# Delta rule: in-place selection instead of mask additions, and another placing of its small steps among the weight products

## The chip, the cores and the metric

The kernel runs on one core of one Trainium2 chip. The metric is the device time of one execution in microseconds. The kernel before takes 3056.31 us (median of three runs, 3056.17 to 3056.36).

## The reference, cut to what matters

Two layers of a hybrid encoder trunk over 256 frames of width 2048, all in float32. Layer 0 mixes forgetting attention and a convolution module, layer 1 is a gated delta rule; each is followed by a SwiGLU feed-forward part. The change touches layer 1 alone. There, for 16 query/key heads and 32 value heads of width 128:

```
q = l2_normalize(q) * HEAD_DIM ** -0.5        # x * rsqrt(sum(x * x) + 1e-6)
k = l2_normalize(k)
decay = exp(where(tril, gcum[:, None] - gcum[None, :], -inf))
lower = where(strict, (k * beta) @ k.T * decay, 0)
a_mat = lower + eye(CHUNK)                    # unit lower triangular
sol   = triangular_solve(a_mat, rhs)
intra = (q @ k.T) * decay
```

## The kernel before, in words

**The weight stream.** Nearly all of the time goes into products with weights from HBM (some 490 MB). They are walked in groups of 512 output columns, each group in four chunks of 1 MB. For each chunk SyncE loads `raw` (L402), ScalarE rounds it in two halves to the short float `w_hi` (L556), VectorE subtracts to get the rest `w_lo` (L902), and TensorE does 16 wide products of `w_hi` with both parts of the activations (L1664) and 16 narrow ones of `w_lo` (L1657). `w_hi` and `w_lo` have two buffers, so the `w_hi` of chunk c + 2 waits until TensorE is through with chunk c. After a group ScalarE copies the second half of each of four accumulators to `tmp` (L563) and VectorE adds the first half (L908); TensorE waits for these sums before it overwrites the accumulators in the next group. For the groups that carry queries, keys and values of the delta rule VectorE then scales by the norm (L967) and does the short convolution in eight portions of two operations (L992, L994), and ScalarE takes the SiLU (L721).

**The delta rule beside it.** The heads are taken in four sets (0 to 3) of four query/key heads and eight value heads. While set j is computed, the stream works through six groups, the gate `z` of set j and the projections of set j + 1 (for set 3 the output projection). Each engine has a generator for the delta rule (`gdn_act`, `gdn_dve`, `gdn_pool`, `gdn_pe`) that is resumed six times in each chunk, so 24 times a group and 144 times a set, at fixed places in the engine's own program; `yield from upto(clock, n)` lets what follows run at the resumption after n. These numbers are called steps below. On TensorE four of the six lie after the 4th, 8th, 12th and 16th wide product, two after the 8th and 16th narrow one (in the last chunk of a group the order is halved: wide, narrow, wide, narrow of eight each). ScalarE and VectorE have their first two steps around the second half of the next chunk's `w_hi` and `w_lo`, the others after it, in the last chunk among the sums. No engine reorders anything: a step that waits holds up everything behind it on its engine.

**What a set does**, with the steps before the change. ScalarE squares queries and keys (L824). TensorE sums the squares over the partitions by products with ones into four PSUM tiles (L1768, steps 4 and 5). ScalarE, in one piece at step 5, takes four logarithms (L830) and one exponential of the whole tile (L834), which makes the reciprocal roots; both need their table loaded. VectorE multiplies queries (step 12), then keys (13) by them (L1321). GpSimd has meanwhile fetched the gate rows, broadcast over the partitions, into `L` and `I` (two DMAs, L1507, 1.5 MB each, after the outputs of the set before were saved), cleared `XT` (L1509), and adds masks of large numbers to two thirds of either (L1512, L1514: four operations of 128x1024). ScalarE takes exponentials of `L` (steps 16 to 23; L841, L842) and `I` (from 24; L851). TensorE makes the products of keys with keys (from step 17; L1776, L1777) and keys with queries (L1860, L1861), VectorE multiplies them into `L` (from 19; L1329, L1331) and `I` (from 28; L1341). GpSimd clears `Xb` and `XTb` (L1517, L1518), moves the diagonal 32x32 blocks of `L` through DRAM to a layout with one block per partition (L1528, L1532), and VectorE inverts them there (`invert`, steps 38 to 62): small operations up to blocks of 16 (L1419 to L1465), then eight large ones of 128x1024 (L1474, L1478, L1483, L1487), one in each step, and a copy (L1492). GpSimd takes the inverses back through DRAM (L1537, L1544, from step 60), VectorE transposes them (L1360, steps 84 to 87), and TensorE works the blocks up to 64 and 128 and finishes the set (from L1805, step 88). VectorE's last product writes the outputs into `zs` (L1398, steps 131 to 134); GpSimd saves them (L1549). For set 3 the saved outputs of the other sets come back as input of the output projection (`og_upper` L586 on ScalarE, `og_lower` L975 on VectorE).

## Time and profile before

| | |
|---|---|
| median of three runs | 3056.31 us (3056.17 to 3056.36) |
| the profiled execution | 3057.1 us, of which its span is 3055.4 us |
| mean granted clock of TensorE | 0.955 |
| TensorE (products) busy | 2817 us, 92% of the span |
| VectorE busy | 1952 us, 64% |
| ScalarE busy | 1402 us, 46% |
| GpSimd busy | 642 us, 21% |
| read from HBM | 491.6 MB, 164 GB/s over the span |

Times in the trace are microseconds from the start of the span. PE is TensorE, PEld its weight loads, DVE VectorE, ACT ScalarE, POOL GpSimd. A row of the timeline merges equal neighbours: start, time from the first's start to the last's end, engine, line, operation, `out<-in`, shapes, count, and in square brackets the idle time before it and what ended it. `x16` is sixteen instructions. PEclk is the granted clock as a share of full speed: 1.00 is 2.4 GHz, 0.50 is 1.2 GHz. The delta rule's four sets run from about 1372 to 2189 us.

### The profile page before, as it was taken

To read this page: it belongs to the slowest core of one execution; us is meant where nothing else is said; L and a number is where in the kernel's file an instruction comes from. 1 tells how busy PE (TensorE), PEld (TensorE's weight loads), DVE (VectorE), ACT (ScalarE), POOL (GpSimd) and SP (SyncE) were. 2 spreads that over 40 slices of the span, in tenths; PEclk is the share of its full clock that TensorE was granted. 3 is DMA by queue.
4 is the path that set the end of the run, shared out by engine and by line. 5 is a ranking of instruction groups with operands and counts; after the bars stand their busy time and mean duration, and the time that the engine had idled before them with its cause. 6 is when DMAs were issued, how large, how long until landed. Compare 5 with 4: busy or idle time off the path is not lost. (4 is left out here: it accounts for less than half of the span.)

```text
span 3055.4 us, 43790 instructions
## 1 busy us (share of the span) xinstructions
PE 2817.2 (92%) x15973; PEld 2463.7 (81%) x15973; DVE 1951.9 (64%) x2454; ACT 1402.3 (46%) x2142; POOL 642.0 (21%) x549
## 2 busy tenths in 40 slices
PE   6966889999999999999888988979899999999997
PEld 5855668888888888877777877968788888888886
DVE  4599647555555555687767668677476555555555
ACT  3555434444444444456355453463444444444443
POOL 4054014011111112411021020031142101210214
PEclk8988879999999999999999999999999999999998
DMA  5533225555555555554444345354455555555553
GB/s 170 165 110 110 97 69 182 191 192 191 181 193 192 185 188 180 172 193 136 131 165 151 119 174 157 120 194 149 139 188 185 187 192 188 186 191 193 181 177 110
DMA packets 246088, 502.26 MB, mean 164 GB/s; under 512 B 10919, under 2 KB 11528, under 8 KB 244392
## 3 DMA queue, kind: packets, MB, share of 16 engines
q1 hardware_dynamic: 237232, 473.99, 47.7%
q0 software_dynamic: 5888, 25.79, 2.4%
q8 instruction: 97, 1.59, 0.2%
q10 hardware_dynamic: 2808, 0.38, 0.1%
q14 instruction: 63, 0.52, 0.0%
HBM read 491.64 MB, written 8.49 MB: 164 GB/s over the span
## 5 line engine op out<-in xcount | busy, mean ns | idle before, releaser
L902 DVE TENSOR_TENSOR w_lo<-raw,w_hi 128x1024 fp32r<-128x1024 f32 (+1 forms) x912 | 1165.9, 1312 | 770.8 <-ACT w_hi L556 770.1
L1664 PE MATMUL acc<-xs,w_hi 128*128 128x512 f32 x5248 | 1333.4, 402 | 59.8 <-ACT w_hi L556 24.3
L556 ACT ACTIVATE w_hi<-raw 128x1024 fp32r<-128x1024 f32 (+1 forms) x912 | 905.4, 1036 | 1011.1 <-PE acc L1657 1002.7
L1664 PEld LDWEIGHTS acc<-xs,w_hi 128*128 128x128 f32 x5248 | 979.1, 194 | 253.2 <-issue 43.4
L1657 PE MATMUL acc<-xs,w_lo 128*128 128x256 f32 x5248 | 719.4, 288 | 63.9 <-DVE w_lo L902 63.9
L1657 PEld LDWEIGHTS acc<-xs,w_lo 128*128 128x128 f32 x5248 | 692.6, 194 | 99.6 <-DVE w_lo L902 70.0
L1664 PE MATMUL acc<-hs,w_hi 128*128 128x512 f32 x1920 | 468.8, 393 | 15.4 <-issue 11.4
L1664 PEld LDWEIGHTS acc<-hs,w_hi 128*128 128x128 f32 x1920 | 352.2, 189 | 83.2 <-issue 13.0
L563 ACT ACTIVATE tmp<-acc 128x256 f32<-128x256 f32 x456 | 172.4, 382 | 338.4 <-PE acc L1657 285.6
L1657 PEld LDWEIGHTS acc<-hs,w_lo 128*128 128x128 f32 x1920 | 251.4, 191 | 12.5
L1657 PE MATMUL acc<-hs,w_lo 128*128 128x256 f32 x1920 | 255.3, 283 | 0.0
L485 POOL TENSOR_TENSOR ut<-gt,ut 128x1024 f32<-128x1024 f32 x22 | 52.9, 2406 | 837.8 <-DVE ut L967 837.8
L908 DVE TENSOR_TENSOR ut<-acc,tmp 128x256 f32<-128x256 f32 x336 | 135.3, 421 | 142.0 <-ACT tmp L563 138.1
L463 POOL TENSOR_TENSOR xT<-xT,ut 128x256 f32 (+1 forms) x140 | 104.1, 766 | 493.9 <-DVE ut L908 493.8
L1219 DVE SCALAR_TENSOR_TENSOR conv<-u_pad,conv_w,conv 128x256 f32<-128x256 f32 x120 | 100.3, 900 | 0.0
L994 DVE SCALAR_TENSOR_TENSOR gt<-ut,short_w,gt 128x255 f32<-128x255 f32 (+2 forms) x192 | 96.9, 563 | 0.2
L1255 POOL TENSOR_TENSOR conv<-conv,prod 128x1024 f32<-128x1024 f32 x30 | 80.2, 2674 | 62.6 <-ACT prod L1244 56.1
L474 POOL TENSOR_TENSOR sq_acc<-sq_acc,sq_one 128x256 f32<-128x256 f32 x60 | 68.8, 1147 | 4.7
L493 POOL TENSOR_TENSOR hs<-ut,hs 128x1024 f32 (+1 forms) x22 | 68.2, 3102 | 5.4 <-POOL hs L490 5.4
L1549 POOL DMA_DIRECT2D og_save<-zs x4 | 3.7, 913 | 295.4 <-DVE zs L1398 295.4
L472 POOL TENSOR_TENSOR sq_one<-xT 128x256 f32 (+1 forms) x60 | 63.6, 1061 | 7.6 <-POOL sq_acc L474 4.1
L908 DVE TENSOR_TENSOR gt<-acc,tmp 128x256 f32<-128x256 f32 x96 | 38.4, 421 | 34.5 <-ACT tmp L563 33.2
(290 smaller groups left out, 1650.4 us busy)
## 6 DMA issues: line engine op xcount, KB each, us to landing
raw<-in_w_in SPq DMA_DIRECT2D x136, 1024.0 KB, 5.2
raw<-in_w_gate SPq DMA_DIRECT2D x88, 1024.0 KB, 5.2
raw<-in_w_up SPq DMA_DIRECT2D x88, 1024.0 KB, 5.2
raw<-in_w_down SPq DMA_DIRECT2D x64, 1024.0 KB, 5.1
raw<-in_w_out SPq DMA_DIRECT2D x48, 1024.0 KB, 5.2
raw<-in_w_down SPq DMA_DIRECT2D x32, 768.0 KB, 4.5
L<-g_rows POOLq DMA_DIRECT2D x4, 1536.0 KB, 7.9
I<-g_rows POOLq DMA_DIRECT2D x4, 1536.0 KB, 11.6
```

The source lines that it names most:

```text
L463: nc.gpsimd.tensor_tensor(row, row, ut[:, m], ALU.add).then_inc(resid_added, 1)
L474: nc.gpsimd.tensor_tensor(sq_acc[:], sq_acc[:], sq_one[:], ALU.add).then_inc(sq_added, 1)
L493: nc.gpsimd.tensor_tensor(hb[:, bass.ds(4 * i, 4), 1, :], ut[:], hi.bitcast(F32), ALU.subtract).then_inc(h_ready, 1)
L556: nc.scalar.activation(w_hi[:, c % 2, k], raw[:, c, k], ACT.Copy).then_inc(hi_ready, 1)
L563: nc.scalar.activation(tmp[:, m % 2], acc[:, m, T:2 * T], ACT.Copy).then_inc(tmp_ready, 1)
L902: nc.vector.tensor_tensor(w_lo[:, c % 2, k], raw[:, c, k], w_hi[:, c % 2, k].bitcast(F32), ALU.subtract).then_inc(lo_ready, 1)
L908: nc.vector.tensor_tensor(dst, acc[:, m, 0:T], tmp[:, m % 2], ALU.add).then_inc(acc_free, 1)
L994: last = nc.vector.scalar_tensor_tensor(gt[:, m, s:T], ut[:, m, 0:T - s], w, gt[:, m, s:T], ALU.mult, ALU.add)
L1219: return eng.scalar_tensor_tensor(conv[:, ct], u_pad[:, ct, k:k + T], w, conv[:, ct], ALU.mult, ALU.add)
L1255: nc.gpsimd.tensor_tensor(conv[:, CONV_DVE:], conv[:, CONV_DVE:], prod[:, k % 2], ALU.add)\
L1657: last = mm(acc[:, m, T:2 * T], w_lo[:, c % 2, k, cols], r[:, kk, 0], start=False, stop=end, skip_group_check=True)
L1664: mm(acc[:, m, :], w_hi[:, c % 2, k, cols], r[:, kk], start=kk == 0, stop=end, skip_group_check=True)
```

## The change

Four things change in the delta rule; all data and results stay where they were.

1. GpSimd selects in place instead of adding masks: `affine_select` over eight heads at a time keeps the triangle and fills the rest with the large number. One operation replaces one addition, four in a set. The constant `mask_up` goes, with its memset and its select at the start.
2. On ScalarE the four logarithms have a step each (8 to 11), and the exponential is split into keys (step 13) and queries (step 14). VectorE multiplies keys at step 15 and queries at step 16, each behind its own half. TensorE's first products of keys are at step 18 instead of 17.
3. In the inverse each of the eight large operations has two steps; the inverse has 33 steps instead of 25 and starts at step 40 instead of 38.
4. What follows is placed two steps later on all engines (the exponentials of `L` and the products into `L` one step). Two places keep their steps: GpSimd's way back through DRAM (60) and VectorE's transposes (84).

The diff, without the hunks that only add 2 to the number in `upto(clock, ...)`:

```
-        mask_up = sb("mask_up", [P, P])
...
-            link(pool.memset(mask_up[:], 0.0))
-            select(mask_up[:], [[1, P]], 0, -1, fill=NEG)
...
             nc.scalar.activation(qk_sq[:], qk_in[:], ACT.Square).then_inc(l2_act, 1)
-            yield from upto(clock, 5)
-
-            act.wait_ge(l2_pe, j + 1)
             for n in range(4):
+                yield from upto(clock, 8 + n)
+                act.wait_ge(l2_pe, j + 1)
                 q = n < 2
                 nc.scalar.activation(qk_sq[:, n // 2, 2 * (n % 2):2 * (n % 2) + 2, :].rearrange("p a t -> p (a t)"),
                                      aux[n][:], ACT.Ln, bias=eps[:, 1:2] if q else eps[:, 0:1],
                                      scale=float(P) if q else 1.0).then_inc(l2_act, 1)
-            act.wait_ge(l2_act, 6 * j + 5)
-            nc.scalar.activation(qk_sq[:], qk_sq[:], ACT.Exp, scale=-0.5).then_inc(l2_act, 1)
+            for n, h in enumerate((1, 0)):
+                yield from upto(clock, 13 + n)
+                act.wait_ge(l2_act, 7 * j + 5)
+                nc.scalar.activation(qk_sq[:, h], qk_sq[:, h], ACT.Exp, scale=-0.5).then_inc(l2_act, 1)
 
             for h in range(SV):
-                yield from upto(clock, 16 + h)
+                yield from upto(clock, 17 + h)
...
         def gdn_dve(dve, j):
...
-            for h in range(2):
-                yield from upto(clock, 12 + h)
-                dve.wait_ge(l2_act, 6 * j + 6)
+            for n, h in enumerate((1, 0)):
+                yield from upto(clock, 15 + n)
+                dve.wait_ge(l2_act, 7 * j + 6 + n)
                 nc.vector.tensor_tensor(qk_in[:, h], qk_in[:, h], qk_sq[:, h], ALU.mult).then_inc(l2_dve, 1)
             for a in range(SQ):
-                yield from upto(clock, 19 + 2 * a)
+                yield from upto(clock, 20 + 2 * a)
...
-            yield from upto(clock, 38)
+            yield from upto(clock, 40)
             for n in range(N_TICKS):
                 next(inverse)
-                if 46 <= clock[0] < 50:
-                    a = clock[0] - 46
+                if 48 <= clock[0] < 52:
+                    a = clock[0] - 48
...
                 link(nc.vector.tensor_tensor(pr, ath[:, 4 * n:4 * n + 4].unsqueeze(2).to_broadcast([P, 4, 16, 16]),
                                              square(Lb, 16, 0, 16).unsqueeze(1).to_broadcast([P, 4, 16, 16]), ALU.mult))
                 yield
+                yield
                 ready()
                 link(nc.vector.tensor_reduce(pt[:, 4 * n:4 * n + 4], pr, AX.X, ALU.add))
+                yield
                 yield
...
             pool.wait_ge(rows_in, 32 * j + 32)
-            for n in (0, 2):
-                nc.gpsimd.tensor_tensor(L[:, :, n], L[:, :, n], over_heads(mask_fox[:]), ALU.subtract).then_inc(gd_pool, 1)
-            for n, mask in ((0, mask_up), (2, mask_up)):
-                nc.gpsimd.tensor_tensor(I[:, :, n], I[:, :, n], over_heads(mask[:]), ALU.add).then_inc(gd_pool, 1)
+            apart(pool)
+            for t, fill, sign in ((L, -NEG, 1), (I, NEG, -1)):
+                for n in (0, 2):
+                    pool.affine_select(out=t[:, :, n], in_=t[:, :, n], compare_op=ALU.is_ge, fill=fill, base=0,
+                                       pattern=[[0, SV], [-sign, P]], channel_multiplier=sign).then_inc(gd_pool, 1)
...
         def gdn_pe(pe, mm, tr, j):
...
             for a in range(SQ):
-                yield from upto(clock, 17 + 2 * a)
+                yield from upto(clock, 18 + 2 * a)
                 pe.wait_ge(l2_dve, 2 * j + 2)
...
             for a in range(2, SQ):
-                yield from upto(clock, 21 + 2 * a)
+                yield from upto(clock, 22 + 2 * a)
                 scores(pe, mm, j, a)
...
-N_CONST = 11
+N_CONST = 9
...
-N_TICKS = 7 + 1 + 3 + 3 + 1 + 1 + 8 + 1
+N_TICKS = 7 + 1 + 3 + 3 + 1 + 1 + 16 + 1
```

The second pair of large operations (L1483, L1487) gets its two further `yield` in the same way.

## Rows read from the trace of the kernel before

**Rows 1.** The page, second part: granted clock of TensorE in 40 slices of 76 us.

```profile
PEclk8988879999999999999999999999999999999998
```

**Rows 2.** Four sets: length; PE, PEld, DVE, ACT, POOL busy; clock, DMA share, GB/s.

```profile
1371.87:1568.68 196.81, 181.55 (x1074) 158.89 (x1073) 143.14 (x239) 100.87 (x187) 14.64 (x22) 0.96 0.43 136
1568.68:1778.96 210.28, 183.56 (x1075) 159.76 (x1073) 154.71 (x244) 101.59 (x188) 28.41 (x29) 0.94 0.46 151
1778.96:1984.90 205.94, 186.21 (x1072) 162.26 (x1073) 145.61 (x237) 100.58 (x185) 27.98 (x29) 0.93 0.45 146
1984.90:2188.90 204.00, 180.10 (x1074) 156.98 (x1072) 138.79 (x196) 100.99 (x187) 40.63 (x43) 0.95 0.50 166
```

**Rows 3.** Timeline of TensorE in set 0, from the inverse to the first use of it.

```profile
1438.93 2.12 PE L1664 MATMUL acc<-xs,w_hi 128*128 128x512 f32 x8 [1.56 <-DVE ut L908]
...
1463.79 2.08 PE L1657 MATMUL acc<-xs,w_lo 128*128 128x256 f32 x8 [4.02 <-DVE w_lo L902]
...
1475.42 3.82 PE L1664 MATMUL acc<-xs,w_hi 128*128 128x512 f32 x16
...
1488.43 1.33 PE L1805 MATMUL aux<-XT,L 128*128 128x64 f32 x8 [2.68 <-DVE X L1360]
```

**Rows 4.** TensorE's waits, 1360 to 2206 us: total, times, longest.

```profile
PE acc L1657 <- DVE w_lo L902: 25.4, 9, 5.5
PE aux L1776 <- DVE qk_in L1321: 23.8, 4, 10.7
PE acc L1664 <- issue: 17.5, 2, 11.4
PE aux L1805 <- DVE X L1360: 9.4, 4, 2.7
PE acc L1664 <- ACT w_hi L556: 8.2, 4, 2.1
PE acc L1664 <- DVE ut L908: 8.1, 6, 2.3
PE aux L1860 <- DVE L L1331: 3.3, 4, 2.1
```

**Rows 5.** Timeline of GpSimd, masks of set 1 and a clearing.

```profile
1585.86 5.88 POOL L1512 TENSOR_TENSOR L<-L,mask_fox 128x1024 f32<-128x1024 f32 x2 [10.09 <-DMA I<-g_rows]
1591.70 5.01 POOL L1514 TENSOR_TENSOR I<-I,mask_up 128x1024 f32<-128x1024 f32 x2
1602.52 0.95 POOL L1517 MEMSET Xb<- 128x1024 f32 x1 [5.81 <-DVE qk_in L1321]
```

**Rows 6.** Timeline of VectorE, the same place in set 0 (first two) and set 1.

```profile
1387.70 2.36 DVE L902 TENSOR_TENSOR w_lo<-raw,w_hi 128x1024 fp32r<-128x1024 f32 x2 [7.97 <-ACT w_hi L556]
1389.98 3.24 DVE L994 SCALAR_TENSOR_TENSOR gt<-ut,short_w,gt 128x255 f32<-128x255 f32 x8
...
1584.90 4.57 DVE L902 TENSOR_TENSOR w_lo<-raw,w_hi 128x1024 fp32r<-128x1024 f32 x2 [7.05 <-ACT w_hi L556]
1589.40 9.56 DVE L994 SCALAR_TENSOR_TENSOR gt<-ut,short_w,gt 128x255 f32<-128x255 f32 x8
```

**Rows 7.** GpSimd's selects at the start (L422): count, ns, start.

```profile
L422 POOL TENSOR_SCALAR_AFFINE_SELECT mask_up<-mask_up x1: 292/292/292, 3.8 to 3.8; 128x128 f32<-128x128 f32 x1
```

**Rows 8.** Groups of GpSimd by shape: count, busy us, mean ns, idle before.

```profile
L490 POOL CAST hs<-ut 128x1024 f32 x16 | 27.5, 1720 | 4.2 <-POOL ut L485 4.2
```

**Rows 9.** Timeline of VectorE beside such a CAST (568.65 to 570.36).

```profile
567.69 3.74 DVE L902 TENSOR_TENSOR w_lo<-raw,w_hi 128x1024 fp32r<-128x1024 f32 x2 [1.79 <-ACT w_hi L556]
```

**Rows 10.** Timeline of ScalarE in set 1, the exponential.

```profile
1580.72 1.28 ACT L834 ACT_TABLE_LOAD   x1
1582.02 1.91 ACT L834 ACTIVATE qk_sq<-qk_sq 128x2048 f32<-128x2048 f32 x1
```

**Rows 11.** Timeline of VectorE in set 0, last copy of the inverse.

```profile
1463.65 0.45 DVE L1492 COPY XTb<-rms 64x128 f32<-64x128 f32 x2
```

**Rows 12.** Transfers of the inverse back to `XT` (L1544).

```profile
DMA to landing us min/median/max: 2.5/3.3/5.9
```

More of the change, by code:

```diff
@@ L845, in gdn_act @@
             for h in range(SV):
-                yield from upto(clock, 24 + (3 * h) // 2)
+                yield from upto(clock, 26 + (3 * h) // 2)
                 if h == 0:
@@ L871, in gdn_act @@
             for a in range(SQ):
-                yield from upto(clock, 120 + a)
+                yield from upto(clock, 122 + a)
                 act.wait_ge(gd_pe[a], NP * j + P_O)
@@ L877, in gdn_act @@
                 last.then_inc(gd_act[a], 1)
-            yield from upto(clock, 125)
+            yield from upto(clock, 127)
             all_heads(act, gd_act, NA * (j + 1))
@@ L1362, in gdn_dve @@
             for a in range(SQ):
-                yield from upto(clock, 94 + a)
+                yield from upto(clock, 96 + a)
                 dve.wait_ge(gd_pe[a], NP * j + P_Z5)
@@ L1381, in gdn_dve @@
             for a in range(SQ):
-                yield from upto(clock, 112 + a)
+                yield from upto(clock, 114 + a)
                 dve.wait_ge(gd_pe[a], NP * j + P_P)
@@ L1387, in gdn_dve @@
             for a in range(SQ):
-                yield from upto(clock, 127 + a)
+                yield from upto(clock, 129 + a)
                 dve.wait_ge(gd_pe[a], NP * j + P_O)
@@ L1765, in gdn_pe @@
             yield from upto(clock, 4)
[L1766 removed]
+            pe.wait_ge(l2_act, 7 * j + 1)
             for n in range(4):
@@ L1789, in gdn_pe @@
             for a in range(SQ):
-                yield from upto(clock, 44 + a)
+                yield from upto(clock, 46 + a)
                 pe.wait_ge(gd_act[a], NA * j + A_LT)
@@ L1797, in gdn_pe @@
             for a in range(SQ):
-                yield from upto(clock, 88 + a)
+                yield from upto(clock, 90 + a)
                 pe.wait_ge(inv_dve, N_INV * j + N_INV)
@@ L1807, in gdn_pe @@
             for a in range(SQ):
-                yield from upto(clock, 92 + a)
+                yield from upto(clock, 94 + a)
                 pe.wait_ge(gd_act[a], NA * j + A_Y5)
@@ L1811, in gdn_pe @@
             for a in range(SQ):
-                yield from upto(clock, 98 + a)
+                yield from upto(clock, 100 + a)
                 pe.wait_ge(gd_dve[a], ND * j + D_X5)
@@ L1819, in gdn_pe @@
             for a in range(SQ):
-                yield from upto(clock, 102 + a)
+                yield from upto(clock, 104 + a)
                 pe.wait_ge(gd_act[a], NA * j + A_Y6)
@@ L1823, in gdn_pe @@
             for a in range(SQ):
-                yield from upto(clock, 106 + a)
+                yield from upto(clock, 108 + a)
                 pe.wait_ge(gd_dve[a], ND * j + D_X6)
```

29 lines of the change are left out of this document (14 added, 15 removed).

## The prediction

> **What bounds the kernel now.** I read the page first: TensorE's granted clock is below full in the first quarter and then, after a steady stretch, through the middle of the span [rows 1], where the delta rule runs. I then cut the stretch of the delta rule, four sets of heads, into windows: each takes 197 to 210 us, and the clock averages 0.93 to 0.96 in them [rows 2]. A set is 24 chunks of weights, and a chunk alone takes TensorE 5.6 us (16 wide products take 3.82 us [rows 3], 16 narrow ones 1.9 us more, less overlap), so some 134 us of each set are weights, the rest is the delta rule's own products and waiting. The seven longest lines of TensorE's waits over this stretch [rows 4] hold 96 us, among them 23.8 us before L1776 (the first product after normalisation), 25.4 us for `w_lo` from VectorE, 8.2 us for `w_hi` from ScalarE, 9.4 us before L1805, 17.5 us of "issue". What the lower clock costs: one minus the clock times the busy time of each set [rows 2] is 7.3 + 11.0 + 13.0 + 9.0 = 40 us, so each us of waiting brings with it 40/96 = 0.4 us of slow matmuls. I use that as a factor. Memory is no bound (DMA share 0.43 to 0.50 [rows 2]).
>
> Two causes stand behind the waits. One is GpSimd: while its four mask additions run (1585.86 to 1596.7 in set 1 [rows 5]), VectorE's second `w_lo` and its short convolution stretch: 9.56 us for eight operations that take 3.24 us in set 0, 4.57 us for two `w_lo` that take 2.36 us there [rows 6]. That is 8.5 us, and in front of L1776 TensorE sat 10.7 us in that set [rows 4]. The other is VectorE itself: in the inverse it is packed without a gap, and the time from 1438.93 to 1463.79 is VectorE's own work, with TensorE waiting 4.02 us at its end [rows 3].
>
> **The change, part by part.**
>
> *Start.* Two constants fewer on GpSimd (a memset and a select of 0.29 us [rows 7], under 0.7 us with their gaps) in GpSimd's first 4.4 us, while the constants' DMAs keep TensorE waiting for longer: nothing, and if that cover were gone, 0.7 us.
>
> *Masks.* Four TENSOR_TENSOR of 128x1024, some 2.7 us each [rows 5], become four selects of one input. The trace has selects of 128x128 only, 0.29 us [rows 7]; a one-input CAST of 128x1024 takes 1.72 us [rows 8]. Bounds for one select: below, the memset's 0.95 us [rows 5]; above, eight times 0.29 = 2.3 us, near a mask addition's shortest. I take the CAST, same size and one input. The trace shows that a CAST holds up VectorE as an addition does (the pair of `w_lo` at 567.69, beside an addition's last 0.7 us and a CAST, takes 3.74 us [rows 9] instead of 2.36), while `w_lo` beside the memset of 1602.52 kept its 1.2 us. The Trainium skill's page "SBUF — State Buffer", section "Who interferes with whom", says the same in a rule that speaks against this change: a VectorE instruction with two SBUF inputs contends with any GpSimd instruction that reads SBUF, and the lock is held for the whole instruction; by it a select still blocks, only for less time. The Trainium skill's "GPSIMD Engine Reference", section "Engine selection", has one-input operations run at roughly line rate, by which a select would take an estimated 1 us instead of 1.7 and the kernel's time would come out near that of the first rival below.
> In set 0 the masks run during the last group before the stretch, and cost TensorE a wait for `w_lo` of 4.7 us (one of the nine in the first line of [rows 4]). With 4 x 1.7 us instead of some 11, VectorE ends its convolution some 2.5 us sooner: gain 2.5 us.
>
> *Logarithms, exponentials, normalisation.* Today all four logarithms and the exponential stand in one block after chunk 0, ahead of the `w_hi` of chunk 2: TensorE waits 2.1 us four times (8.2 us [rows 4]). With logarithms in steps 8 to 11, both halves of that `w_hi` are out first: this wait goes. What is late next: the new chain through chunk 2 begins when TensorE ends chunk 1 and frees the buffer: `w_hi` 1.05, table load 1.28, exponential of the keys 1.0 (half of 1.91 [rows 10] and a fixed part), `w_hi` 1.05, `w_lo` 1.2, two taps 0.8 [rows 6], product of the keys 1.21, two taps 0.8, product of the queries 1.21: 9.6 us. TensorE is at its new step (18) after 5.57 + 1.0 = 6.6 us. So a wait of 3.0 us is left before L1776 even with GpSimd silent; nothing gets faster there, since the products moved three steps later on VectorE and the user only one on TensorE. Queued behind the wait are the weights of chunk 3; behind ScalarE's new waits stand only later `w_hi` with room to spare. Splitting the exponential adds 0.2 us of ScalarE, hidden.
> In sets 1 to 3 the selects begin 14 to 17 us after the set's start, as the masks do now (the row DMAs gate them), and this chain runs 15 to 25 us after it. So they no longer meet a convolution with slack, but the chain itself. Two of four falling on it add 3.4 us (from 0 to 4 x 1.72 possible). New waits: 3.0 + 3 x 6.4 = 22.2 us against 8.2 + 23.8 + 3.3 (L1860, which starts one step later with its operands no later) = 35.3 us [rows 4]: gain 13.1 us.
> Clock on these 15.6 us of waits: 0.4 x 15.6 = 6.3 us.
>
> *Inverse.* The eight large operations (1.22 us each) get two steps each, the whole starts two steps later, the last copy ten steps later. The work is the same and VectorE sets the pace, so little vanishes: stepping through chunks, steps 49 to 72 hold 31 us of VectorE for 22 us of TensorE. Today TensorE reaches the second chunk of the next group (1475.42) 40.2 us after it entered the stretch (1435.2, which is 1438.93 less the wait and eight products before it [rows 3]); placed by the new steps I get waits of 1.2, 1.9, 1.2, 0.6 and 1.9 us and 35.7 us, 4.5 us better, because VectorE no longer idles behind its own late `w_lo` and the small operations start the sums earlier. But the inverse itself ends at 33 us instead of 28.9 (1463.65 and 0.45 [rows 11]): **4 us later**. From there the blocks go through DRAM; GpSimd's waits and issues take 9 us of that, the last landing 3.3 us (up to 5.9) more [rows 12], some 13 us together. VectorE then stands at its step 84 waiting 1.6 to 3.4 us, with `w_lo` of the next chunk queued behind, and L1805 starts at 51.7 to 53.5 us, two steps (1.9 us) further on in the work than today's 53.2 (1488.43 [rows 3]): a net 1.6 to 3.4 us. I take 2.5 us for sets 0 to 2, clock included. In set 3 the two loads of stored heads stand between (6.0 us of the "issue" line of [rows 4] at the first): gain at the first of them, loss at the second, 0 in all.
>
> *Everything after moves by two steps*, on all engines alike. That is free until the end of a set: the last product with `zs` gates the save of the heads, GpSimd's. In sets 1 to 3 the row DMAs and selects start some 1.5 us later (counted above), and after set 3 the chain of save, load, ScalarE and VectorE that ends TensorE's longest "issue" wait, 11.4 us [rows 4], starts and ends about 1 us later: loss 1 us.
>
> **Sum.** 2.5 + 13.1 + 6.3 + 3 x 2.5 - 1 = 28.4 us. The profiled execution took 3057.1 us (span 3055.4), which gives 3028.7 us; the median of the runs stands 0.8 us below it: **3028 us**, 0.9% faster. A measurement of this kernel can tell about 0.2%, 6 us, from no change.
>
> **Rivals.**
> *The lock costs nothing* (20%): selects as short as the memset's 0.95 us [rows 5], mostly between VectorE's operations. Waits 4 x 3.0 = 12 us, gain 23.3; nearly all of the 4.7 us before set 0, 4.3; clock 0.4 x 27.6 = 11; inverse 3 x 4.5 if the blocks land early; less 1: 51 us, 3005 us. For: GpSimd's memsets disturb no one. Against: the CAST does.
> *Selects scale with their columns* (18%): 8 x 0.29 = 2.3 us each, that is 0.6 us more for up to four blocked operations in four places, with the clock 1.4 x 16 x 0.6 = 13 us: 3042 us.
> *The blocks' way through DRAM becomes the bound* (13%): landings of 5.9 us, waits of 5.5 us at L1805 with slow matmuls behind: the 7.5 us are gone and 3 more: 3039 us. GpSimd's code being fetched anew before the first select of a set would land near 3045 us. The start of the trace speaks against that: its selects follow their memsets within 0.3 us.
> *Slower* (7%): a select over eight heads in a strided tile takes a slow path and holds the lock all through. Each us above 1.7 costs 1.4 x 16 = 22 us; from 3.0 us a select the gain is gone, at 3.5 us the kernel takes 3067 us. Against: 0.29 us for 128 columns.
> *It does nothing* (4%): a packed VectorE merely passes its lateness on to another line: 3056 us.
> The forecast's own case has 38%. Range for eight in ten: 3005 to 3048 us, which leaves out the fast half of the first rival and the last two. Faster by over 0.2%: 0.88; within: 0.05; slower: 0.07.
>
> **What would show it.** GpSimd's selects near 1.7 us; no 2.06 us waits for `w_hi`; waits before L1776 of about 3 us in set 0 and 5 to 7 us in sets 1 to 3, with taps or the product at 2 us instead of 0.4 and 1.2; the last copy of the inverse 4 us later against the group's start, and VectorE waiting for a DMA before L1360; set lengths falling by about 7 us on average, set 1 most. The forecast is wrong if selects exceed 3 us, or if TensorE's waits in this stretch add up to over 95 us again.

## The result, and the profile after

The changed kernel takes **3023.37 us** (median of four runs, 3020.1 to 3027.0) against 3056.24 us for the kernel before beside it: a ratio of 0.990, 95% interval 0.9889 to 0.9912. That is 33 us faster where 28 were forecast. The profiled execution took 3021.7 us, its span 3020.2 us, at a mean granted clock of 0.962. In the text "L1777", "L1806" and the like are lines of the changed kernel; before they were L1776, L1805 and so on, one to three lines further up or down.

The four sets, as in [rows 2] (length; PE, PEld, DVE, ACT, POOL busy; clock, DMA share, GB/s):

```profile
1362.90:1555.96 193.06, 179.88 (x1072) 156.61 (x1073) 143.37 (x240) 102.38 (x188) 14.69 (x22) 0.97 0.45 142
1555.96:1751.50 195.54, 179.52 (x1074) 156.08 (x1073) 146.53 (x243) 102.78 (x189) 23.83 (x29) 0.97 0.48 160
1751.50:1955.22 203.72, 183.89 (x1072) 159.70 (x1073) 146.06 (x238) 101.95 (x187) 24.02 (x29) 0.95 0.46 150
1955.22:2155.07 199.85, 181.86 (x1074) 158.67 (x1072) 131.52 (x196) 101.97 (x188) 34.31 (x43) 0.96 0.50 167
```

They are 3.8, 14.7, 2.2 and 4.2 us shorter than before, 25 us in all. The stretch also begins 9.0 us sooner (1362.9 instead of 1371.9), of which one wait accounts for 4.7 (below); the start of the stretch differs by some 5 us between two profiles of the changed kernel. TensorE's waits (total, times, longest), to be read against [rows 4]:

```profile
PE aux L1777 <- DVE qk_in L1319: 14.9, 4, 4.6
PE acc L1665 <- issue: 10.3, 1, 10.3
PE acc L1665 <- DVE ut L906: 9.5, 9, 1.5
PE aux L1855 <- DVE os L1389: 8.7, 4, 2.4
PE aux L1806 <- DVE X L1358: 8.2, 4, 4.0
PE acc L1658 <- DVE w_lo L900: 8.1, 6, 1.9
PE aux L1861 <- DVE L L1329: 7.0, 8, 1.4
PE acc L1665 <- ACT w_hi L553: 3.8, 1, 3.8
```

Three things stand out. The waits for `w_lo` fell from 25.4 to 8.1 us, those before the first product of keys from 23.8 to 14.9. The first scores (L1861) wait more than before (7.0 instead of 3.3). And there is a line that no row of before has: **8.7 us before L1855**, the transposes of the outputs. All of TensorE's waits in this view add up to 101.0 us before and 77.4 us after. Of the 35 us between the two profiles, 24 are thus waits. Over sets 0 to 2, cut at the first sum of squares of each, the length fell from 613.4 to 592.3 us, the idle times in the timeline from 61.1 to 49.0, and TensorE's busy time, for the same products, from 551.6 to 543.3, at a mean granted clock of 0.965 instead of 0.942. Most of what is left of the 35 us lies ahead of the stretch.

The selects, and VectorE beside them, in set 1 (timelines, as [rows 5, 6]):

```profile
1571.48 3.13 POOL L1514 TENSOR_SCALAR_AFFINE_SELECT L<-L 128x1024 f32<-128x1024 f32 x2 [9.64 <-DMA I<-g_rows]
1574.57 3.12 POOL L1514 TENSOR_SCALAR_AFFINE_SELECT I<-I 128x1024 f32<-128x1024 f32 x2
```

```profile
1572.00 1.66 DVE L900 TENSOR_TENSOR w_lo<-raw,w_hi 128x1024 fp32r<-128x1024 f32 x1 [1.66 <-ACT w_hi L553]
1575.32 1.41 DVE L900 TENSOR_TENSOR w_lo<-raw,w_hi 128x1024 fp32r<-128x1024 f32 x1 [1.66 <-ACT w_hi L553]
1576.66 1.70 DVE L992 SCALAR_TENSOR_TENSOR gt<-ut,short_w,gt 128x253 f32<-128x253 f32 x2
1578.28 1.21 DVE L1319 TENSOR_TENSOR qk_in<-qk_in,qk_sq 128x1024 f32<-128x1024 f32 x1
```

A select of 128x1024 has a record of 1.6 us here (means: 1.64 us on `L`, 1.53 us on `I`), against 2.8 and 2.7 us for an addition. VectorE lost 0.4, 0.2 and 0.8 us to them and was free when the product of the keys came.

These means are not the work of a select. In each pair above one took 1.09 us and the other 2.07, and the long ones began while VectorE was in the middle of a `w_lo`. Minimum, median and maximum in ns, of the changed kernel and of the one before:

```profile
L1514 POOL TENSOR_SCALAR_AFFINE_SELECT L<-L x8: 1088/1828/2073, 1348.0 to 1972.2; 128x1024 f32<-128x1024 f32 x8
L1512 POOL TENSOR_TENSOR L<-L,mask_fox x8: 2357/2674/3382, 1350.8 to 2002.5; 128x1024 f32<-128x1024 f32 x8
```

The run with the selection alone (below) has a set where VectorE stands idle beside them, and there all four take 1.08 or 1.09 us:

```profile
1779.71 2.13 POOL L1509 TENSOR_SCALAR_AFFINE_SELECT L<-L 128x1024 f32<-128x1024 f32 x2 [8.22 <-DMA I<-g_rows]
1781.80 2.12 POOL L1509 TENSOR_SCALAR_AFFINE_SELECT I<-I 128x1024 f32<-128x1024 f32 x2
```

Two additions beside an idle VectorE take 2.39 and 2.41 us (set 2 before). So the two engines wait for each other in turn: a tap takes 1.30 us beside selects (0.43 by itself), and a select 1.27 us beside taps and up to 2.08 beside a `w_lo`.

### The profile page after: what moved, and what is told of

It is laid out like the page before. It is cut to its first block and busy times, and to the rows that moved or that the text cites. A ratio compares the mean times of both kernels' runs of the same rounds, so it can differ in the third digit from the quotient of the medians.

```text
span 3020.2 us, 43811 instructions
## 1 busy us (share of the span) xinstructions
PE 2805.7 (93%) x15973; PEld 2452.0 (81%) x15973; DVE 1932.1 (64%) x2454; ACT 1407.1 (47%) x2146; POOL 622.0 (21%) x547
## 5 line engine op out<-in xcount | busy, mean ns | idle before, releaser
L1665 PE MATMUL acc<-hs,w_hi 128*128 128x512 f32 x1920 | 468.5, 393 | 14.3 <-issue 10.3
L1665 PEld LDWEIGHTS acc<-hs,w_hi 128*128 128x128 f32 x1920 | 352.1, 189 | 82.0 <-issue 11.9
L992 DVE SCALAR_TENSOR_TENSOR gt<-ut,short_w,gt 128x255 f32<-128x255 f32 (+2 forms) x192 | 86.0, 504 | 0.2
```

The source lines that it names most:

```text
L992: last = nc.vector.scalar_tensor_tensor(gt[:, m, s:T], ut[:, m, 0:T - s], w, gt[:, m, s:T], ALU.mult, ALU.add)
L1665: mm(acc[:, m, :], w_hi[:, c % 2, k, cols], r[:, kk], start=kk == 0, stop=end, skip_group_check=True)
```

## The experiments

Twelve kernels ran, in three groups, each beside the kernel before, which stood at 3054.4, 3054.1 and 3054.6 us; so medians can be compared across groups. One kernel's own runs spread over 3 to 10 us (over 16 in the one with half the spacing), the interval of a ratio is about 0.0015 to either side, some 4.5 us; a difference of two kernels below some 6 us is therefore not sure. The last two columns are of the one profiled execution: length of sets 0 to 2 with TensorE's busy time in it, and the sum of TensorE's waits from 1355 to 2206 us. Where the profiles differ ahead of the stretch, no edit below is the cause, other than the wait of 4.7 us.

| kernel | median us | ratio, interval | sets 0 to 2, busy | waits |
|---|---|---|---|---|
| before | 3056.24 | | 613.4, 551.6 | 101 |
| changed | 3023.37 | 0.9900 (0.9889 to 0.9912) | 592.3, 543.3 | 77 |
| the change again | 3024.35 | 0.9900 (0.9885 to 0.9915) | 588.0, 541.3 | 77 |
| additions back | 3044.03 | 0.9970 (0.9958 to 0.9982) | 599.6, 544.6 | 95 |
| roots block back | 3030.62 | 0.9926 (0.9912 to 0.9939) | 594.7, 542.7 | 83 |
| one step each in the inverse | 3015.75 | 0.9876 (0.9861 to 0.9891) | 585.0, 533.1 | 80 |
| `o_rs` early | 3020.45 | 0.9885 (0.9870 to 0.9900) | 589.1, 541.1 | 78 |
| before, with selection alone | 3033.22 | 0.9932 (0.9918 to 0.9945) | 603.8, 548.2 | 87 |
| selects twice | 3034.81 | 0.9937 (0.9923 to 0.9951) | 600.2, 545.4 | 91 |
| `o_rs` and `os` early | 3013.04 | 0.9871 (0.9856 to 0.9887) | 583.9, 537.1 | 72 |
| before, with selection and roots | 3039.08 | 0.9944 (0.9931 to 0.9957) | 606.1, 551.7 | 85 |
| one step each, `o_rs` and `os` early | 3016.69 | 0.9872 (0.9858 to 0.9887) | 586.9, 538.2 | 75 |
| the same, keys two steps later | 2999.59 | 0.9821 (0.9808 to 0.9833) | 574.5, 532.8 | 65 |
| half spacing, `o_rs` and `os` early | 3027.53 | 0.9902 (0.9886 to 0.9917) | 599.8, 544.6 | 83 |

**The change again**, the base of the second group:

> The changed kernel unchanged, measured on the same chip as the three others of this group, as their base. It stood at 3023.4 us beside 3056.2 of the kernel before, a ratio of 0.990: 3021 to 3025 us is expected, if the chip's own kernel before is near 3055.

3024.35 us. Set 2 took 196.2 us here against 199.8 in the first profile (both from first sum of squares to the next), with a wait before L1806 of 0.8 us instead of 4.0: this wait depends on when a DMA lands, and it varies from execution to execution (the section on the spacing says why).

### What the selection brings

```diff
+            for n in (0, 2):
+                nc.gpsimd.tensor_tensor(L[:, :, n], L[:, :, n], over_heads(mask_fox[:]), ALU.subtract)...
+            for n, mask in ((0, mask_up), (2, mask_up)):
+                nc.gpsimd.tensor_tensor(I[:, :, n], I[:, :, n], over_heads(mask[:]), ALU.add)...
-                    pool.affine_select(out=t[:, :, n], in_=t[:, :, n], ...
```

> The changed kernel (3023.4 us) with the four mask additions and the constant mask_up back in place of the four selects; everything else as changed. Theory A (the prediction's: an operation of GpSimd on two thirds of L or I holds VectorE up for its whole length): four operations of some 2.7 us instead of 1.6 us, and this time beside the chain of table load, exponential, w_hi, w_lo, taps and product. The wait of 4.7 us for w_lo before set 0 comes back; in sets 1 to 3 the wait before the first product of keys grows from 4 us to 9 to 11 us: 4.7 + 3 x 6 = 23 us, with slow matmuls 1.4 x 23 = 32 us, so about 3055 us. Theory B (the selects brought little beyond set 0; the gain is the new placing of logarithms and exponentials): that wait grows by 2 us at most in each of sets 1 to 3: 1.4 x (4.7 + 6) = 15 us, about 3038 us.

It took 3044.03 us: the additions cost 20 us. TensorE's timeline, before set 0 and at the first product of keys in sets 1 to 3:

```profile
1364.79 2.08 PE L1662 MATMUL acc<-xs,w_lo 128*128 128x256 f32 x8 [4.71 <-DVE w_lo L903]
...
1592.37 0.79 PE L1781 MATMUL aux<-qk_in 128*128 128x128 f32 x2 [8.59 <-DVE qk_in L1322]
...
1796.85 0.80 PE L1781 MATMUL aux<-qk_in 128*128 128x128 f32 x2 [5.91 <-DVE qk_in L1322]
...
2000.28 0.80 PE L1781 MATMUL aux<-qk_in 128*128 128x128 f32 x2 [9.51 <-DVE qk_in L1322]
```

The 4.7 us came back whole, and the others grew by 4.5, 2.8 and 4.9 us over the changed kernel's 4.1, 3.1 and 4.6. VectorE's timeline of set 1 shows where it loses them, to be set beside the rows with selects above:

```profile
1578.42 2.53 DVE L903 TENSOR_TENSOR w_lo<-raw,w_hi 128x1024 fp32r<-128x1024 f32 x1 [1.71 <-ACT w_hi L556]
1581.74 2.55 DVE L903 TENSOR_TENSOR w_lo<-raw,w_hi 128x1024 fp32r<-128x1024 f32 x1 [0.79 <-ACT w_hi L556]
1584.22 5.04 DVE L995 SCALAR_TENSOR_TENSOR gt<-ut,short_w,gt 128x253 f32<-128x253 f32 x2
```

Two taps, 0.87 us by themselves, take 5.04 us beside additions and 1.70 beside the end of the selects. The measured time lies between the two theories; 17 us more waiting came with 20 us more time, where theory A's factor asks for 24 (the difference is within the interval).

> The kernel before with one part of the change only: four selects in place of four mask additions, mask_up gone; all steps as before. Theory A (the selection's gain is its own and does not hang on the placing): the wait of 4.7 us before set 0 goes, and the waits before the first product of keys, 0.6, 10.7, 3.9 and 8.6 us, fall to what the run with the old roots block showed with selects, 0 to 0.6, 5.1, 2.2 and 4.0 us: 4.7 + 12 = 17 us, with slow matmuls 20 to 24 us: 3031 to 3035 us. Theory B (most of what the additions cost was hidden by the old placing, and they only hurt where the new placing puts the chain beside them): 5 to 12 us, 3043 to 3050 us.

3033.22 us, 21 us below the kernel before: theory A. The waits before the first product of keys were 2.2, 5.6, 2.2 and 5.5 us. Undoing the selection costs 20 us, doing it alone gives 21. It is two thirds of the whole gain and needs nothing else of the change.

Does a select still hold VectorE up? Each select was done twice:

```diff
-            for t, fill, sign in ((L, -NEG, 1), (I, NEG, -1)):
+            for t, fill, sign, turn in ((L, -NEG, 1, 0), (L, -NEG, 1, 1), (I, NEG, -1, 0), (I, NEG, -1, 1)):
+                if turn:
+                    pool.wait_ge(gd_pool, NO * j + (3 if t is L else 7))
```

> The changed kernel with each of the four selects of a set done twice (the second leaves the same values), 6.5 us more of GpSimd reading and writing SBUF per set, beside the chain of exponential, w_hi, w_lo, taps and product. Theory A (a select holds VectorE up for its whole length): some 3 to 5 us more wait before the first product of keys in each of sets 1 to 3 and 2 us before set 0: 14 us, with slow matmuls 20 us: about 3042 us. Theory B (a select of some 1.6 us holds VectorE up for a third of its length or less): 1 us a set, 3026 us.

3034.81 us, 10.5 us slower than the changed kernel beside it, between the two again; in its profile, which is its slowest execution (3043.7 us), the wait before the first product of keys grew from 14.7 to 24.8 us and the waits for `w_lo` from 8.1 to 11.1. VectorE's timeline in set 1, while selects run from 1580.58 to 1592.75:

```profile
1584.41 1.68 DVE L900 TENSOR_TENSOR w_lo<-raw,w_hi 128x1024 fp32r<-128x1024 f32 x1 [1.66 <-ACT w_hi L553]
1586.02 2.53 DVE L992 SCALAR_TENSOR_TENSOR gt<-ut,short_w,gt 128x253 f32<-128x253 f32 x2
1588.47 2.10 DVE L1319 TENSOR_TENSOR qk_in<-qk_in,qk_sq 128x1024 f32<-128x1024 f32 x1
```

Each of these VectorE operations is longer by up to the rest of a select: two taps 2.53 instead of 0.87, a product 2.10 instead of 1.21. So the select blocks as an addition does, operation by operation. It costs less because it is shorter (1.09 us of its own instead of 2.4) and because in the changed kernel the four of set 1 are over, at 1577.7, before VectorE comes to the product of the keys at 1578.3.

### What the placing of the roots brings

The old block (four logarithms and one exponential at step 5, products at 12 and 13, keys at 17, `L` exponentials from 16, products into `L` from 19) went back, all else as changed:

> The changed kernel with the four logarithms and one exponential back in one block at step 5, the normalising products at steps 12 and 13, the first products of keys at 17, the exponentials of L from 16, products into L from 19; selects, inverse and all later steps as changed. Theory A: the new placing is what moved the waits of 8.2 us for w_hi; they come back, while the wait before the first product of keys, no longer lengthened by additions, falls from the changed kernel's 14.9 us in four sets to about 4 (1 us each, as in set 0 of the kernel before), and the waits at the first scores from 7.0 to about 4: net change 8.2 - 11 - 3 = -6 us, times 1.4: about 3015 us. Theory B (the placing carries the gain): with the block back the waits before the first product stay at 4 us in sets 1 to 3 and 8.2 us come on top: about 3035 us.

3030.62 us, 6 to 7 us slower than the two measurements of the changed kernel, just about what the runs can tell: nearer to theory B. The waits for `w_hi` came back, 2.06 us four times, and the waits before the first product of keys did not vanish (total 11.9 us, for 14.9 with the new placing):

```profile
PE acc L1664 <- ACT w_hi L553: 14.3, 6, 3.8
PE aux L1776 <- DVE qk_in L1318: 11.9, 4, 5.1
```

The placing was then added to the kernel before with the selection, without the move of all later steps by two:

> The kernel before with two parts of the change: the selection, and the new placing of logarithms, exponentials and normalising products (L exponentials from 17, products of keys from 18, into L from 20). The inverse (one step each, from 38) and everything behind it keep the steps of before. Selection alone gave 21 us (3033 us). Theory A (parts add up; the placing is worth what its undoing cost, 7 to 9 us, and the move of all later steps by two costs the 8.7 us wait for os, so leaving it out gains): 3033 - 8 = 3025 us or less; with no wait before the transposes of os. Theory B (the new placing only pays together with the later start of the inverse, for which VectorE is too late otherwise): 3033 us or more, with the waits for w_lo and sums in the inverse grown.

3039.08 us: not 8 us faster than the selection alone but 6 us above it, theory B's side, though not for the reason it gave. The 6 us are at the edge of what the runs can tell, and 3.7 of the 5.6 us between the profiles lie ahead of the stretch; what is sure is that nothing is gained. The waits for `w_hi` are gone (no such line is left), but the scores now wait:

```profile
PE aux L1857 <- DVE L L1329: 16.1, 8, 2.6
```

ScalarE's timeline shows why. The exponentials of `L` (from step 17) and those of `I` (still from 24) meet at step 24, and the second half of a `w_hi` stands behind them; VectorE's `w_lo` and its last products into `L` follow at 1408.42 and 1410.70, TensorE at 1412.14 after a wait of 2.60 us:

```profile
1405.59 1.85 ACT L849 ACTIVATE I<-I,gate_n 128x128 f32<-128x128 f32 x6
1407.34 1.05 ACT L553 ACTIVATE w_hi<-raw 128x1024 fp32r<-128x1024 f32 x1
```

This wait of 2.60 us comes four times, once a set. The kernels that have the selection and differ only in the other parts, side by side (medians in us):

| | later steps as before | later steps moved by two |
|---|---|---|
| roots as before | 3033 | 3031 (with the spacing) |
| roots placed anew | 3039 | 3016 (without the spacing), 3023 and 3024 (with it) |

The right and the left kernel of the second row, 3039 and 3016 us, differ in nothing but part 4 of the change and the start of the inverse at 40 instead of 38. **The move of all later steps by two is thus worth some 23 us beside the new roots**, although it brings a new wait of 8.7 us (below). The scores wait 9.0 us instead of 16.1, and the transposed blocks of the inverse 2.4 instead of 9.4; but all waits together fell only from 85 to 80 us, and most of the gain is in TensorE's busy time, 533.1 us in sets 0 to 2 instead of 551.7 at a granted clock of 0.974 instead of 0.946. Why the clock is so much better there no run shows. So the new placing of the roots pays only together with the later steps; which of them is needed (the `I` exponentials, the inverse) was not tried one by one, nor was the move without the new roots and without the spacing.

### What the spacing of the inverse brings

```diff
                 yield
-                yield
...              (four such lines in all)
-N_TICKS = 7 + 1 + 3 + 3 + 1 + 1 + 16 + 1
+N_TICKS = 7 + 1 + 3 + 3 + 1 + 1 + 8 + 1
```

> The changed kernel with one step for each of the eight large operations of the inverse again (25 steps from step 40). Theory A (the prediction's): worth 2.5 us in each of sets 0 to 2; with it gone TensorE waits up to 4 us at the end of the stretch for w_lo, and 1.4 us more than now on the whole: 3029 to 3032 us. Theory B (VectorE is the pace in either placing and merely passes its lateness on): within 2 us of 3023.

3015.75 us, some 8 us faster than the changed kernel; neither theory had that. TensorE in set 0, first with two steps each (the changed kernel), then with one:

```profile
1441.48 2.17 PE L1658 MATMUL acc<-xs,w_lo 128*128 128x256 f32 x16 [0.83 <-DVE w_lo L900]
...
1447.40 1.21 PE L1658 MATMUL acc<-xs,w_lo 128*128 128x256 f32 x8 [1.91 <-DVE w_lo L900]
...
1452.48 1.17 PE L1665 MATMUL acc<-xs,w_hi 128*128 128x512 f32 x4 [1.08 <-DVE ut L906]
...
1456.58 3.31 PE L1665 MATMUL acc<-xs,w_hi 128*128 128x512 f32 x8 [1.52 <-DVE ut L906]
```

```profile
1445.46 2.18 PE L1654 MATMUL acc<-xs,w_lo 128*128 128x256 f32 x16 [0.81 <-DVE w_lo L900]
...
1455.02 2.07 PE L1654 MATMUL acc<-xs,w_lo 128*128 128x256 f32 x8 [5.54 <-DVE w_lo L900]
```

The waits in the stretch are nearly the same in sum, 5.5 (with one of 0.2 not shown) against 6.4 us; the spacing cuts one long wait into several. (In set 0 TensorE reached L1806 107.4 us after the first sum of squares with two steps each, 108.5 with one: the spacing gains 1 us there.) From the start of the chunk at step 48 to the second chunk of the next group TensorE needs 40.5 us in the kernel before, 39.0 with selection and roots, and 37.3 in both of these: that gain comes with either spacing. What also differs is what follows: with one step each the wait before the transposed blocks are used is 0.8 us in sets 0 to 2 and none worth a line in set 3, and VectorE never waits for a DMA there. With two it is 0.8, 1.1, 4.0 and 2.3 us. VectorE's timeline of the changed kernel in set 2, and what waited for the DMA over all sets:

```profile
1865.53 0.70 DVE L1358 STREAM_TRANSPOSE X<-XT 32x512 f32<-32x512 f32 x1 [2.77 <-DMA XT<-x_diag]
```

```profile
  DVE X L1358: 8.3, 2
```

From the end of the last copy of the inverse to the first transpose (step 84) there are 15 us with one step each (sets 0 to 2), in which the blocks always arrived. With two there are 11.6 in set 0; in set 2 the blocks needed 13.1. In set 2 the products after that wait run slow: eight of 128x64 take 1.97 us instead of 1.10, and the set's busy time is 183.7 us instead of 177.7. But the wait is not what makes the set slow: in the change again it is 0.8 us there, and the busy time is 182.9 us all the same.

Over all four sets TensorE's waits for `w_lo`, for the sums and for the transposed blocks add up to 38.2 us before (without the 4.7 us ahead of set 0), 31.6 with selection and roots, 25.8 in the changed kernel and 25.4 with one step each. The spacing only moves waits from one line to another. All waits together are 80 us with one step each and 77 with two; the 8 us between the medians are therefore not waits but busy time (533.1 us against 543.3 and 541.3 in sets 0 to 2), and no run shows why.

> As b1, but the first four of the eight large operations of the inverse have two steps and the last four one (29 steps from step 40): the inverse ends four steps earlier than in the changed kernel and four later than in b1. Theory A (the spacing itself is worth 1 to 2 us a set, as the two first sets of the changed kernel show against the run with one step each, and the loss comes only from the blocks' way through DRAM, for which four steps of slack suffice): 2 to 6 us faster than b1, about 3001 us. Theory B (VectorE's lateness is merely spread over several short waits, and the short waits bring a slow clock): between b1 and the kernel with os early alone, 3005 to 3013 us.

3027.53 us, 11 us slower than one step each, on theory B's side and beyond its range. The inverse did not end sooner for its four steps fewer: the last copy came 89.5 us after the set's first sum of squares (89.2 with the full spacing, 86.8 with none), so in set 0 VectorE's own work sets the pace and not the step. And the blocks took longer on their way (13.8 us in set 0, 15.3 in set 2), since the transfer to DRAM landed after 3.9 us (median) instead of 2.1:

```profile
PE aux L1804 <- DVE X L1358: 12.1, 3, 4.9
```

Why does it take twice as long at some moments (also 4.2 us in the kernel before, 2.1 with one step each from 40)? No run was made for this, but all fourteen traces show one pattern: it goes by how long before the transfer SyncE issued a weight load of 1 MB (`raw`). Kernel before, then the changed kernel:

```profile
1463.89 0.37 SPq L402 DMA_DIRECT2D raw<-in_w_in  x1
1464.69 1.58 POOL L1537 DMA_DIRECT2D x_diag<-XTb  x3 [42.72 <-DVE XTb L1492]
```

```profile
1453.63 0.37 SPq L401 DMA_DIRECT2D raw<-in_w_in  x1
1457.80 1.59 POOL L1538 DMA_DIRECT2D x_diag<-XTb  x3 [44.88 <-DVE XTb L1494]
```

In the four kernels with slow transfers (before, selection alone, selection and roots, half spacing) the first of a set's three is issued 0.8 to 1.3 us after such a load and lands after 3.9 to 4.5 us, in all sixteen sets. In the ten others it is issued 3.3 to 4.3 us after one, when most of that load is over, and lands after 1.9 to 2.3 us, in all forty sets. The loads back into `XT` do the same: the eighteen that are issued up to 1.5 us after a weight load need 5.3 to 6.4 us, the sixteen that are issued less than 0.3 us ahead of one 3.8 to 6.0, and of the 145 that are further away on both sides (over 1.5 us behind one, over 1 us ahead of the next) all but two need 2.2 to 4.2. Set 2 of the changed kernel fits this: its last load back is issued at the same moment as the next weight load and lands after 5.7 us, while in the change again the weight load comes 1.3 us later and the block lands after 2.2.

### The new wait for the outputs

The two steps by which everything moved also have a price. `o_rs` went from the end of a chunk (125) to between the halves of the next `w_hi` (127), and VectorE's `os` from between the halves of `w_lo` (127) to behind both and two taps (129). First `o_rs` alone was put back to 125:

> The changed kernel with ScalarE's logarithm and exponential of the outputs' squares (o_rs) directly behind the fourth square at step 125 instead of step 127, where they stand between the two halves of a w_hi. In the changed kernel TensorE waits 2.40, 2.34, 2.34 and 1.61 us before the transposes of the outputs (8.7 us in all), which the kernel before does not. Theory A (the two steps brought this wait): it goes, and with it the slow matmuls behind it: 1.2 to 1.4 x 8.7 = 10 to 12 us, 3011 to 3013 us. Theory B (it is the VectorE's or the clock's lateness that shows there and goes to the next line, w_lo or the next w_hi): 3020 to 3024 us.

3020.45 us, 3 to 4 us faster, not more than the interval: theory B's time. The wait itself fell from 8.7 to 6.1 us only. Then `os` too:

```diff
-            yield from upto(clock, 127)
+            yield from upto(clock, 125)
             all_heads(act, gd_act, NA * (j + 1))
...
-                yield from upto(clock, 129 + a)
+                yield from upto(clock, 127 + a)
                 dve.wait_ge(gd_pe[a], NP * j + P_O)
                 dve.wait_ge(rms_o, 2 * j + 2)
```

> The changed kernel with o_rs at step 125 (as in the run before) and, in addition, VectorE's products of the outputs with it (os) from step 127 instead of 129; TensorE's transposes of them stay at 131. With o_rs early alone TensorE still waited 1.7 us in sets 0 to 2, since os then stands behind the second half of w_lo and two taps. Theory A: the products now come between the two halves of w_lo, 2.0 us earlier, and the wait of 8.7 us in all goes: against the changed kernel beside it, 8 to 12 us faster. Theory B (the halves of w_lo and the taps are late by as much as os was early, and the next w_lo or w_hi takes over the wait): 0 to 3 us faster.

3013.04 us, 11 us faster: theory A. The wait is gone, but other waits grew by 4 us (all together 72 instead of 77), so the waits alone do not make 11 us; the busy time in sets 0 to 2 fell by 4. VectorE in the changed kernel, then with this edit, and last the line of TensorE's waits that is left:

```profile
1538.70 1.23 DVE L900 TENSOR_TENSOR w_lo<-raw,w_hi 128x1024 fp32r<-128x1024 f32 x1 [2.87 <-ACT w_hi L553]
1539.84 0.87 DVE L992 SCALAR_TENSOR_TENSOR gt<-ut,short_w,gt 128x255 f32<-128x255 f32 x2
1540.63 0.68 DVE L1389 TENSOR_TENSOR os<-aux,o_rs 128x512 f32<-128x512 f32 x1
```

```profile
1538.47 1.23 DVE L900 TENSOR_TENSOR w_lo<-raw,w_hi 128x1024 fp32r<-128x1024 f32 x1 [8.20 <-ACT w_hi L553]
1539.62 0.68 DVE L1389 TENSOR_TENSOR os<-aux,o_rs 128x512 f32<-128x512 f32 x1
1540.22 1.22 DVE L900 TENSOR_TENSOR w_lo<-raw,w_hi 128x1024 fp32r<-128x1024 f32 x1
```

```profile
PE aux L1855 <- DVE os L1389: 0.3, 2, 0.2
```

### Together

> The changed kernel with both improvements seen so far: one step for each large operation of the inverse (alone 6 to 8 us faster than the changed kernel), and o_rs at 125 with os from 127 (alone 11 us faster). Theory A (they lie in different groups of the set and add up): 18 us below the changed kernel's 3024, about 3005 us. Theory B (both are gains in the same slow clock or the same lateness): 3010 to 3013 us, as the better one alone.

3016.69 us: theory B. The two gains (8 and 11 us) don't add up. In its profile both waits are gone, but others grew: `w_hi` 7.4 us instead of 3.8, `ut` up to 2.7 instead of 1.1, and in set 2 matmuls ran slow (181.9 us busy against 177.7 with one step each alone). Seen from here the spacing costs nothing (3013.0 with it, 3016.7 without, within what the runs can tell), where the pair before said 8 us, which lay in busy time and not in waits. What holds in both is that it gains nothing.

> As the kernel before it in this group, and in addition TensorE's products of keys from step 20 instead of 18, its last scores from 24 + 2a, and VectorE's products into L from 22 instead of 20. TensorE waits 3.1 to 5.7 us before the first product of keys (16 us in four sets). Two steps are 1.9 us of TensorE's work. Theory A (the wait is the chain's lateness and shrinks by what the user moves): 4 x 1.9 = 8 us less wait, with slow matmuls 8 to 11 us: about 2996 us. Theory B (the products into L and I and the start of the inverse get late in turn: GpSimd sends L out two steps later, and the inverse, at step 40, waits for it): 0 to 4 us gained, or a loss.

**2999.59 us**, 17 us below the kernel without this step, 24.8 below the change, 55 below the kernel before (ratio 0.982): theory A, and more. The edit:

```diff
-                yield from upto(clock, 18 + 2 * a)
+                yield from upto(clock, 20 + 2 * a)
                 pe.wait_ge(l2_dve, 2 * j + 2)
...
-                yield from upto(clock, 22 + 2 * a)
+                yield from upto(clock, 24 + 2 * a)
                 scores(pe, mm, j, a)
...
-                yield from upto(clock, 20 + 2 * a)
+                yield from upto(clock, 22 + 2 * a)
                 dve.wait_ge(gd_pe[a], NP * j + P_KK)
```

```profile
PE aux L1773 <- DVE qk_in L1319: 9.3, 4, 3.8
PE aux L1857 <- DVE L L1329: 5.1, 6, 1.0
```

The first line was 16.6 us in the run without the step, the second 7.5. Over sets 0 to 2 the busy time fell by another 5.4 us (538.2 to 532.8), the clock's share (0.965 to 0.979). The edit was tried on this kernel only, not on the changed one. The inverse, at the same step 40, waits for nothing new (its last copy, by GpSimd's issue behind it, is at 84.2 us after the set's first sum of squares, 87.9 without).

## Why the prediction was right, and where it was not

The forecast, 3028 us, and its sign held, and 3023 lies well inside the range. But the sum is right for reasons that are only in part its own.

- **Masks before set 0** (forecast 2.5 us): the wait of 4.7 us went whole, as the additions brought it back whole.
- **Price of a select** (1.72 us, from a CAST): the means are 1.64 and 1.53 us, but this match is luck. A select's own work is 1.09 us; the rest of its record is waiting for VectorE. The CAST was no clean measure either: each of the 22 CASTs began while a `w_lo` was running, and ended 0.9 us after that `w_lo`. The "roughly line rate" of the Trainium skill, "GPSIMD Engine Reference", section "Engine selection", from which 1 us was estimated, fits the 1.09 us.
- **A select still holds VectorE up**: right. In the doubled run a product took 2.10 us instead of 1.21. By the Trainium skill, "SBUF — State Buffer", section "Who interferes with whom", a VectorE instruction with two SBUF inputs contends with a GpSimd instruction that reads SBUF, and the trace agrees, in both directions.
- **Roots, keys and scores** (35.3 to 22.2 us forecast): measured 14.9 + 7.0 = 21.9 us, a match by two errors. The step "Two of four falling on it add 3.4 us" failed: over the 3.1 us of set 0 the waits were longer by 1.0, 0 and 1.5 us; in set 1 the selects had ended at 1577.7 and the first product came at 1578.3. And the step that let the 3.3 us of the first scores vanish failed: they became 7.0. The 3.0 us forecast for set 0 were 3.14.
- **No 2.06 us waits for `w_hi`**: held. That this placing is a gain by itself was wrong: with the later steps left where they were it gains nothing (3039 us against 3033).
- **Clock** (0.4 us for each us of waiting): over sets 0 to 2 it was 8.3 us of busy time for 12.1 of waits, near 0.7; with the additions back the kernel lost 20 us for 17 of waits; and one step each in the inverse had 2 to 3 us more waits with 8 to 10 us less busy time. One factor for all waits does not hold, and what sets the clock here stays open. (Its term is also misrounded: 0.4 x 15.6 is 6.2, not 6.3.)
- **Inverse** (gain 7.5 us): the gain is there, its reason was wrong. In set 0 the five waits of the stretch were forecast as 1.2, 1.9, 1.2, 0.6 and 1.9 us and came as 0.8, 1.9, 1.1, 0.2 and 1.5, and the way to the second chunk of the next group became 3.2 us shorter (forecast 4.5). But the kernel with one step each from step 40 has the same 37.3 us for it: what failed is the step that put this down to the spacing, for the forecast compared with the old start at 38 only (39.0 us there with selection and roots). The rival that the way through DRAM becomes the bound took place in sets 2 and 3 (waits of 4.0 and 2.3 us, VectorE idle 8.3 us for two landings).
- **"Everything after moves by two steps, on all engines alike. That is free until the end of a set"**: this step failed most clearly, in both directions. The steps do not lie evenly around `w_hi` and `w_lo`; moved by two, `os` came behind the second half of `w_lo`, and TensorE waited 8.7 us. The run without that wait is 11 us faster. And the move was no mere consequence of the other parts: beside the new roots it is worth 23 us net, for which the sum has no term.
- **End** (loss 1 us): the last "issue" wait was 10.3 us, not 11.4, and the first one of 6.0 us became one of 3.8 us for `w_hi`.

So the selection by itself gives 21 of the 33 us, undone it costs 20: this part is shown. The other parts together add some 9 us. They are no sum: the new roots and the later steps pay only together (17 us, with one step each in the inverse), and the spacing took 8 of these back in that comparison and nothing in the other. That the forecast's terms came to the right total is in good part luck. The first rival (the lock costs nothing) is out, since the doubled selects cost 10 us; only its short select, 0.95 us, was nearly right.

## What to carry to other kernels

A GpSimd operation that reads SBUF beside a busy VectorE is paid for on VectorE, operation by operation; here sixteen operations, each shorter by some 1.3 us of its own work, gave 20 us, about their whole sum, although GpSimd is busy for a fifth of the time only. The duration in a profile of such an operation contains the wait for the other engine: look for one that ran beside an idle engine before you use it as a price. In a schedule written out as steps, moving everything by the same number is no neutral act (here it brought 23 us net, in spite of a new wait of 8.7 us): look for each moved operation at what it now stands behind on its own engine. And when a consumer waits at its step in every round, try first to move the consumer: two steps later for TensorE's keys gave 17 us here, more than the 9 us of everything in the change but the selection. And parts of a schedule should be measured in pairs, not only one by one: several expectations above failed because gains did not add up.

## What the runs showed of the hardware

- A GpSimd select in place of 128x1024 (float32) takes 1.09 us beside an idle VectorE, an addition of the same size 2.35 to 2.41 us. Beside a VectorE operation with two inputs in SBUF both engines wait for each other, one operation at a time: a select takes 1.27 us beside taps and up to 2.08 beside a `w_lo`, an addition 2.5 to 2.6 and up to 3.4.
- VectorE pays per operation, so small ones suffer most: two taps of 0.43 us each took 5.04 us beside additions, 2.56 us each.
- Transfers of 64 and 128 KB to DRAM on GpSimd's queue land after 1.9 to 2.3 us when they are issued 3.3 to 4.3 us after a weight load of 1 MB, and after 3.9 to 4.5 us when they are issued 0.8 to 1.3 us after one (first transfer of each set, fourteen traces). That the weight load is the cause was not tried by a run of its own.
